# Feed-forward gate and up by Strassen's seven products, over pairs of weight chunks and two groups of tokens

## The chip, the cores and the metric

The kernel runs on one core of one Trainium2 chip. The metric is the device time of one execution in microseconds, here the median of three runs. The engines of the core work side by side and wait for each other through semaphores: PE (TensorE, matrix products), DVE (VectorE), ACT (ScalarE), POOL (GpSimd), and SP (SyncE), which here only issues DMAs.

## The reference

Two layers of an encoder run over 1168 tokens: 1024 of a prompt, 128 of eight running streams and 16 meta tokens. Each layer projects the input, attends in two groups of heads, mixes, and ends with a dense feed-forward part. The change is in that last part alone:

```python
x = layer_norm(ALPHA * x + jnp.einsum('btm,md->btd', mix, w_out), ln1_g, ln1_b)
hid = jax.nn.silu(jnp.einsum('btd,df->btf', x, wg)) * jnp.einsum('btd,df->btf', x, wu)
return layer_norm(ALPHA * x + jnp.einsum('btf,fd->btd', hid, wd), ln2_g, ln2_b)
```

Here `x` is 1168 x 1024, `wg` and `wu` are 1024 x 2816 and `wd` is 2816 x 1024, all in 32 bits.

## The kernel before

Every product of float32 matrices is made of three matmuls in the type float32r, in the helper `three` (lines 2426, 2427 and 2428): each operand is held as a high part, rounded to float32r, and a remainder ("hi" and "lo"), and high x high, high x remainder and remainder x high are added up in PSUM. The first operand that `three` is given is loaded as weights, 128 x 128, the second is moved through. High parts are made by copies on ACT, remainders by subtraction (original minus high part) on POOL or DVE.

The tokens lie transposed, as `xh` and `xl`, 128 features to a partition, in KD = 8 blocks of 1168 columns. The 2816 hidden features are FC = 22 chunks of 128. A turn of the feed-forward loop takes two chunks. For each chunk gate and up are computed for three groups of tokens, N0 and NT (390, 390, 388 columns), each over the eight feature blocks (`up_or_gate`). The results of gate lie in three banks of PSUM and those of up in three others. ACT makes silu of the gate (line 1771), DVE multiplies it by up (line 2359), ACT rounds the product into `hidh` (line 1776), DVE makes `hidl` (line 2363).

Down (`down`) takes both chunks of the turn before: 8 blocks of output by 3 groups of tokens give 24 units of 6 matmuls. Units take turns on the two banks `Tb`; DVE adds each to `acc` in SBUF (line 2381, in the first turn line 2372 with the factor ALPHA). A unit waits for the addition of the unit two before it (semaphore `f_y`).

The order is written out by hand on each engine. On PE a turn is: gate of chunk 0, the down units of the turn before, then up of chunk 0, gate and up of chunk 1. Six weight tiles of 512 KB come for every turn in the order TURN_ITEMS; ACT makes the high part (`weights_hi`), POOL the remainder (`w_lo`, line 1343: 1024 elements to a partition). Of DVE's 36 operations of a turn only the six `hidl` ones read two tensors in SBUF; the others read PSUM and SBUF.

The attention stages ahead use the same split. Line 2116 (DVE) rounds probabilities, and lines 2120 (DVE) and 1288 (POOL) make the two halves of their remainders at the same time, each from two tensors in SBUF.

Of the kernel before, what the change touches and what calls it, by code (L numbers as in the profile page):

```python
# [9 lines left out]
ALU = mybir.AluOpType  # L10
# [86 lines left out]
X_GROUPS = ((0, 1, 2), (3, 4, 5), (6, 7), (8, 9))  # L97
# [167 lines left out]
def program(nc, X, LNP, ROT, W_IN, QKVG, W_UQ, W_UK, W_UV, SINKS, MIXG, W_OUT, LN1, W_FF,  # L265
# [7 lines left out]
    with ExitStack() as ctx:  # L273
# [228 lines left out]
        xh = m("xh", [P, KD, TOK], F32R)  # L502
        xl = m("xl", [P, KD, TOK], F32R)
        after_x = m.at
# [9 lines left out]
        m = Map(common)  # L514
        m.at = after_x
        acc = m("acc", [P, KD, TOK])

        hidh, hidl, fwh, fwl = [None] * 2, [None] * 2, [None] * 6, [None] * 6
        for i in range(2):
            hidh[i], hidl[i] = m(f"hidh{i}", [P, TOK], F32R), m(f"hidl{i}", [P, TOK], F32R)  # L520

        late_end = win_at + W_LATE * 4 * INW
        fwh[4] = m("fwh4", [P, KD, P], F32R)
        assert m.at <= late_end
        for i in range(2):
            fwh[i], fwl[i] = m(f"fwh{i}", [P, KD, P], F32R), m(f"fwl{i}", [P, KD, P], F32R)
        gate = m("gate", [P, TOK])
        fwh[2], fwl[2] = m("fwh2", [P, KD, P], F32R), m("fwl2", [P, KD, P], F32R)
        assert m.at >= win_at + KD * 4 * INW
        fwl[4] = m("fwl4", [P, KD, P], F32R)  # L530
        fwh[5], fwl[5] = m("fwh5", [P, KD, P], F32R), m("fwl5", [P, KD, P], F32R)
        assert m.at <= win_at + (KD + W_LATE) * 4 * INW
        fwh[3], fwl[3] = m("fwh3", [P, KD, P], F32R), m("fwl3", [P, KD, P], F32R)
        fraw = [raw[0][:, 0:D].rearrange("p (k f) -> p k f", f=P), raw[1][:, 0:D].rearrange("p (k f) -> p k f", f=P),
                m("fraw2", [P, KD, P])[:, :, :]]

# [157 lines left out]
        LAST_T = (11, 13, 15, 19, 21, 23)  # L694
        LAST_STATS = (12, 14, 16, 20, 22, 23)
# [3 lines left out]
        def last_bank(e):  # L699
            return (Tb[0], Tb[1], PS[:, 2 * BANK:3 * BANK], PS[:, 5 * BANK:6 * BANK])[e % 4]  # L700
# [232 lines left out]
        def _(sp):  # L933
            for l in range(L):
# [19 lines left out]
                if l >= 1:  # L954
# [4 lines left out]
                    sp.wait_ge(S("f_lo"), W_ITEMS * l)  # L959
# [2122 lines left out]
```

## Time and profile before

| | |
|---|---|
| median of three runs | 3252.19 us (3252.14 to 3256.39) |
| span of the profiled execution | 3254.4 us |
| PE busy | 3060.8 us, 94% |
| DVE, ACT, POOL busy | 1445.3, 895.4 and 835.9 us |
| feed-forward stretch of layer 1, about 2362 to 3226 us | 864 us |

Busy times are sums over the span; an engine that is busy for 44% of it can still be the one that another waits for in some stage. Matmuls are pipelined: a row's duration is longer than the distance from its start to the next one's, which is what a sequence of them costs.

### The profile page before, as it was taken

To read this page: it belongs to the slowest core of one execution; us is meant where nothing else is said; L and a number is where in the kernel's file an instruction comes from. 1 tells how busy PE (TensorE), PEld (TensorE's weight loads), DVE (VectorE), ACT (ScalarE), POOL (GpSimd) and SP (SyncE) were. 2 spreads that over 40 slices of the span, in tenths; PEclk is the share of its full clock that TensorE was granted. 3 is DMA by queue.
4 is the path that set the end of the run, shared out by engine and by line. 5 is a ranking of instruction groups with operands and counts; after the bars stand their busy time and mean duration, and the time that the engine had idled before them with its cause. 6 is when DMAs were issued, how large, how long until landed. Compare 5 with 4: busy or idle time off the path is not lost. (4 is left out here: it accounts for less than half of the span.)

```text
span 3254.4 us, 46316 instructions
## 1 busy us (share of the span) xinstructions
PE 3060.8 (94%) x18352; PEld 2792.0 (86%) x18352; DVE 1445.3 (44%) x2763; ACT 895.4 (28%) x1726; POOL 835.9 (26%) x684
## 2 busy tenths in 40 slices
PE   7979998999999999999889699989899999999997
PEld 6956666878999999999889566678699999999996
DVE  6657776653222222222454677766422222222225
ACT  3333344434111111111233344354431111111111
POOL 2323343421111211111432234434121111111113
PEclk9979998999999999999989899989999999999998
DMA  4321115633111111110232212065321111111101
GB/s 169 131 74 48 40 34 163 181 106 115 39 45 39 39 45 39 39 39 26 105 107 98 73 43 56 18 206 170 103 89 46 39 39 39 39 39 39 39 26 72
DMA packets 143826, 235.36 MB, mean 72 GB/s; under 512 B 52528, under 2 KB 93744, under 8 KB 143376
## 3 DMA queue, kind: packets, MB, share of 16 engines
q1 hardware_dynamic: 133120, 202.48, 19.5%
q0 software_dynamic: 10576, 31.14, 2.5%
q8 instruction: 84, 1.38, 0.2%
q14 instruction: 46, 0.38, 0.0%
HBM read 179.13 MB, written 50.38 MB: 71 GB/s over the span
## 5 line engine op out<-in xcount | busy, mean ns | idle before, releaser
L2427 PE MATMUL PS<-xl,fwh 128*128 128x390 f32 (+1 forms) x2112 | 721.9, 342 | 0.0
L2426 PE MATMUL PS<-xh,fwh 128*128 128x390 f32 (+1 forms) x2112 | 720.3, 341 | 0.6
L2428 PE MATMUL PS<-xh,fwl 128*128 128x390 f32 (+1 forms) x2112 | 720.7, 341 | 0.0
L2381 DVE TENSOR_TENSOR acc<-acc,PS 128x390 f32<-128x390 f32 (+1 forms) x432 | 241.7, 560 | 420.8 <-PE PS L2428 420.8
L2359 DVE TENSOR_TENSOR gate<-PS,gate 128x390 f32<-128x390 f32 x132 | 74.3, 563 | 739.7 <-PE PS L2428 739.7
L2426 PEld LDWEIGHTS PS<-xh,fwh 128*128 128x128 f32 x2112 | 399.1, 189 | 3.1 <-DVE xl L2279 2.5
L2427 PEld LDWEIGHTS PS<-xl,fwh 128*128 128x128 f32 x2112 | 398.5, 189 | 0.4
L2428 PEld LDWEIGHTS PS<-xh,fwl 128*128 128x128 f32 x2112 | 398.6, 189 | 0.0
L2426 PE MATMUL PS<-hidh,fwh 128*128 128x390 f32 (+1 forms) x1056 | 359.0, 340 | 5.2 <-DVE hidl L2363 4.5
L2428 PE MATMUL PS<-hidh,fwl 128*128 128x390 f32 (+1 forms) x1056 | 360.5, 341 | 0.0
L2427 PE MATMUL PS<-hidl,fwh 128*128 128x390 f32 (+1 forms) x1056 | 358.9, 340 | 0.0
L1776 ACT ACTIVATE hidh<-gate 128x390 fp32r<-128x390 f32 x132 | 70.0, 531 | 990.6 <-DVE gate L2359 990.6
L1343 POOL TENSOR_TENSOR fwl<-raw,fwh 128x1024 fp32r<-128x1024 f32 x82 | 195.8, 2397 | 544.2 <-ACT fwh L1788 446.8
L1288 POOL TENSOR_TENSOR Pl<-Pf,Ph 128x256 fp32r<-128x256 f32 (+5 forms) x174 | 219.0, 1265 | 393.3 <-DVE Ph L2116 393.3
L1343 POOL TENSOR_TENSOR fwl<-fraw,fwh 128x1024 fp32r<-128x1024 f32 x42 | 100.4, 2391 | 774.9 <-ACT fwh L1793 674.5
L1587 ACT ACTIVATE Pf<-PS 128x512 f32<-128x512 f32 (+5 forms) x174 | 127.6, 752 | 284.4 <-PE PS L2535 283.9
L2426 PEld LDWEIGHTS PS<-hidh,fwh 128*128 128x128 f32 x1056 | 199.0, 188 | 6.4 <-issue 5.0
L2428 PEld LDWEIGHTS PS<-hidh,fwl 128*128 128x128 f32 x1056 | 199.7, 189 | 0.0
L2427 PEld LDWEIGHTS PS<-hidl,fwh 128*128 128x128 f32 x1056 | 198.7, 188 | 0.0
L2426 PE MATMUL PS<-winh,xTh 128*128 128x394 f32 (+3 forms) x480 | 170.4, 355 | 9.6 <-DVE xTl L1863 5.6
L2427 PE MATMUL PS<-winl,xTh 128*128 128x394 f32 (+3 forms) x480 | 166.3, 347 | 0.0
L2428 PE MATMUL PS<-winh,xTl 128*128 128x394 f32 (+3 forms) x480 | 166.1, 346 | 0.0
(442 smaller groups left out, 5364.3 us busy)
## 6 DMA issues: line engine op xcount, KB each, us to landing
raw<-in_W_FF SPq DMA_DIRECT2D x88, 512.0 KB, 3.3
fraw<-in_W_FF SPq DMA_DIRECT2D x44, 512.0 KB, 3.2
sqt_scratch<-sqTs POOLq DMA_DIRECT2D x18, 512.0 KB, 4.6
hc<-out_H SPq DMA_DIRECT2D x18, 512.0 KB, 3.5
out_H<-yo POOLq DMA_DIRECT2D x18, 512.0 KB, 3.0
dkraw<-in_CKVT SPq DMA_DIRECT2D x16, 520.0 KB, 4.5
QS<-sqt_scratch SPq DMA_DIRECT2D x16, 512.0 KB, 3.4
mt<-mix_scratch SPq DMA_DIRECT2D x16, 512.0 KB, 4.7
```

The source lines that it names most:

```text
L1288: ins = pool.tensor_tensor(Pl[i][0:kk, 1, c], Pf[i][0:kk, 1, c], f(Ph[i][0:kk, 1, c]), ALU.subtract)
L1343: pool.tensor_tensor(fwl[dst][:, :, :], fraw[slot], f(fwh[dst][:, :, :]), ALU.subtract)\
L1587: ins = act.activation(Pf[r][0:kk, :, c], both_banks(u)[0:kk, :, c], ACT.Exp)
L1776: act.activation(hidh[c][:, N0[i]:N0[i] + NT[i]], gate[:, N0[i]:N0[i] + NT[i]], ACT.Copy)\
L2359: dve.tensor_tensor(g, u_bank(i), g, ALU.mult).then_inc(S("f_hid"), 1)
L2381: dve.tensor_tensor(a, a, Tb[e % 2][:, 0:NT[i]], ALU.add).then_inc(S("f_y"), 1)
L2426: pe.matmul(out, wh, mh, start=start, stop=False)
L2427: pe.matmul(out, wh, ml, start=False, stop=False)
L2428: return pe.matmul(out, wl, mh, start=False, stop=stop)
```

## The change

Gate and up are no longer computed chunk by chunk. A pair is now chunk p and chunk p + 11. The weights of a pair are seen as a 2 x 2 matrix of blocks (two halves of the 1024 features by two chunks), the tokens as another (two halves of a group's tokens by two halves of the features). Strassen's form (Winograd's variant) then gives the four blocks of the result from seven products of half-size blocks instead of eight. Its operands are X_OP and W_OP: some are blocks, the others (S1 to S4, T1 to T4) sums and differences of blocks, made on DVE. Every operand is split into a high part and a remainder after it has been summed.

The tokens are in two groups, of 512 and 656, so matmuls move half a group, 256 or 328 columns. All eleven pairs are run for the first group, then all for the second, 22 turns in all; the weights are loaded, summed and split anew for each. A turn has 14 products of 4 x 3 matmuls (7 of gate, 7 of up) in the banks BANK_OF, and 16 down units of 6 matmuls for the turn before. All 16 stand behind product 6, between gate and up (DOWN_STEPS). The x operands of the second group are made in turns 10 and 11, in the places of those of the first.

On DVE `product_sum` and `quarter_sum` add products in PSUM to partial sums in SBUF (`sum_u`, `upper`, `gate`) and multiply up by silu of gate; `w_sum` makes T1 to T4 for gate and for up; `hid_lo` makes the remainders of hid in two operations. On POOL `w_lo` and `down_lo` make 18 remainders of 512 elements a turn. BANK_READER names the DVE operation after which a product's bank is free.

On DVE, in the feed-forward loop of before (`hidl` is the remainder of hid, `acc` the sum in SBUF, `PS` any PSUM):

```order
L2363 TENSOR_TENSOR hidl0_260<-gate_268,hidh0_259 128x390 [waits f_hidh] x2
L2363 TENSOR_TENSOR hidl0_260<-gate_268,hidh0_259 128x388 [waits f_hidh]
L2359 TENSOR_TENSOR gate_268<-PS,gate_268 128x390 [waits f_up,f_silu] x2
L2359 TENSOR_TENSOR gate_268<-PS,gate_268 128x388 [waits f_up,f_silu]
...
L2381 TENSOR_TENSOR acc_258<-acc_258,PS 128x390 [waits f_down]
...
L2381 TENSOR_TENSOR acc_258<-acc_258,PS 128x390 [waits f_down]
...
L2381 TENSOR_TENSOR acc_258<-acc_258,PS 128x388 [waits f_down]
```

and in the loop of the first token group after, from the second up product on (`T1` to `T4` are the weight sums, `rg0` and `rg1` hold the pair's gate weights for the next turn; the T3 row reads two halves of `rg1`):

```order
L2604 TENSOR_TENSOR upper_294<-PS,sum_u0_291 128x256 [waits f_acted,f_prod]
...
L2607 TENSOR_TENSOR gate_295<-upper_294,gate_295 128x256 [waits f_acted]
...
L2562 TENSOR_TENSOR T1_302<-rg1_312,rg0_311 128x512 [waits f_g_in]
...
L2562 TENSOR_TENSOR T2_303<-rg1_312,T1_302 128x512 [waits f_t]
L2580 TENSOR_TENSOR sum_u1_292<-PS,sum_u0_291 128x256 [waits f_prod]
...
L2562 TENSOR_TENSOR T3_308<-rg1_312 128x512 [waits f_g_in,f_lo]
...
L2583 TENSOR_TENSOR sum_u2_293<-PS,sum_u1_292 128x256 [waits f_made]
...
L2562 TENSOR_TENSOR T4_309<-rg0_311,T2_303 128x512 [waits f_t]
...
L2604 TENSOR_TENSOR upper_294<-PS,sum_u2_293 128x256 [waits f_made]
...
L2607 TENSOR_TENSOR gate_295<-upper_294,gate_295 128x256 [waits f_acted]
```

Between two sums out of PSUM now stand operations that read SBUF alone. In the same place before stood additions to `acc` only, each behind a wait for its down unit.

On POOL, one turn of before (`fraw`, `raw` hold raw weights):

```order
L1343 TENSOR_TENSOR fwl0_265<-raw1_69,fwh0_264 128x1024 [waits f_hi]
...
L1343 TENSOR_TENSOR fwl4_271<-fraw2_276,fwh4_263 128x1024 [waits f_hi]
...
L1343 TENSOR_TENSOR fwl5_273<-raw0_68,fwh5_272 128x1024 [waits f_hi]
...
L1343 TENSOR_TENSOR fwl1_267<-raw1_69,fwh1_266 128x1024 [waits f_hi]
...
L1343 TENSOR_TENSOR fwl2_270<-fraw2_276,fwh2_269 128x1024 [waits f_hi]
...
L1343 TENSOR_TENSOR fwl3_275<-raw0_68,fwh3_274 128x1024 [waits f_hi]
```

and part of a turn after, from the first up product on (`wopl` is the remainder of a product's weights, `wdl` that of down):

```order
L1470 TENSOR_TENSOR wopl0_279<-rg0_311,woph0_278 128x512 [waits f_hi]
...
L1470 TENSOR_TENSOR wopl1_281<-rg0_311,woph1_280 128x512 [waits f_hi]
...
L1470 TENSOR_TENSOR wopl2_283<-T2_303,woph2_282 128x512 [waits f_hi]
...
L1477 TENSOR_TENSOR wdl_297<-rd0_310,wdh_296 128x512 [waits f_dhi]
...
L1477 TENSOR_TENSOR wdl_297<-rd1_305,wdh_296 128x512 [waits f_dhi]
...
L1470 TENSOR_TENSOR wopl3_285<-T1_302,woph3_284 128x512 [waits f_hi]
...
L1470 TENSOR_TENSOR wopl4_287<-T3_308,woph4_286 128x512 [waits f_hi]
...
L1470 TENSOR_TENSOR wopl5_299<-T4_309,woph5_298 128x512 [waits f_hi]
...
L1470 TENSOR_TENSOR wopl6_301<-rg1_312,woph6_300 128x512 [waits f_hi]
...
L1470 TENSOR_TENSOR wopl0_279<-ru0_306,woph0_278 128x512 [waits f_hi]
```

Six operations of 1024 elements a turn have become eighteen of 512, four of them (`wdl`, in two pairs) between the weights of the products.

On PE, the first down unit of before:

```order
L2426 MATMUL PS<-xh_248,fwh3_274 128x388 [waits f_hid]
L2427 MATMUL PS<-xl_249,fwh3_274 128x388
L2428 MATMUL PS<-xh_248,fwl3_275 128x388
L2426 MATMUL PS<-xh_248,fwh3_274 128x388
L2427 MATMUL PS<-xl_249,fwh3_274 128x388
L2428 MATMUL PS<-xh_248,fwl3_275 128x388
L2426 MATMUL PS<-xh_248,fwh3_274 128x388
```

and the end of the seventh product and the first two and a half down units after:

```order
L2730 MATMUL PS<-xoh6_254,woph6_300 128x256 [waits f_acted]
L2731 MATMUL PS<-xol6_261,woph6_300 128x256
L2732 MATMUL PS<-xoh6_254,wopl6_301 128x256
...
L2730 MATMUL PS<-hidh_289,wdh_296 128x256 [waits f_made]
L2731 MATMUL PS<-hidl_290,wdh_296 128x256
L2732 MATMUL PS<-hidh_289,wdl_297 128x256
L2730 MATMUL PS<-hidh_289,wdh_296 128x256
L2731 MATMUL PS<-hidl_290,wdh_296 128x256
L2732 MATMUL PS<-hidh_289,wdl_297 128x256
L2730 MATMUL PS<-hidh_289,wdh_296 128x256 [waits f_y]
```

The unit's own shape is the same, two chunks of three matmuls; it is 256 columns wide, and the third one, 12 matmuls on, waits for the first addition (`f_y`).

The diff, cut to its core; the constants, then POOL's turn:

```diff
-TURNS = FC // 2
-TURN_ITEMS = [(1, 0, 0), (0, 0, 2), (0, 1, 2), (1, 0, 1), (1, 1, 0), (1, 1, 1)]
-NT = (390, 390, 388)
-N0 = (0, 390, 780)
+PAIRS = FC // 2
+TURNS = 2 * PAIRS
+PRODUCTS = 14
+DOWNS = 16
+G_TOKENS = (4 * P, TOK - 4 * P)
+HALF_G = (G_TOKENS[0] // 2, G_TOKENS[1] // 2)
+X_OP, W_OP = ("A11", "A12", "S2", "S1", "S3", "A22", "S4"), ("B11", "B21", "T2", "T1", "T3", "T4", "B22")
+BANK_OF = (0, 1, 2, 3, 4, 5, 0, 1, 2, 3, 4, 5, 2, 3)
+DOWN_STEPS = (6,) * 16
...
+                def turn(j, c, downs=True, ahead=True):
+                    for i in range(PRODUCTS):
+                        if i < 7 or ahead:
+                            w_lo(j, c, i + 7)
+                        if i == 1 and downs:
+                            down_lo(j - 1, c, 1)
+                        if i == 9:
+                            down_lo(j, c, 0)
```

ACT's copies of the weights:

```diff
+                def w_hi(j, c, i, first=False):
+                    w, k = i // 7, i % 7
+                    if not first:
+                        act.wait_ge(S("f_prod"), Q(j, c, PRODUCTS, i - 6))
...
+                    if name[0] == "T":
+                        act.wait_ge(S("f_t"), Q(j, c, 8, 4 * w + int(name[1])))
```

DVE:

```diff
+                def hid_lo(j, c, g):
+                    for h in (1, 0):
+                        dve.wait_ge(S("f_acted"), acted(j, c, "hi1" if h else "hi0"))
+                        dve.tensor_tensor(hidl[:, :, half_of(g, h)], gate[:, :, half_of(g, h)],
+                                          f(hidh[:, :, half_of(g, h)]), ALU.subtract).then_inc(S("f_made"), 1)
+                def product_sum(j, c, g, i):
...
+                    if m == 2:
+                        dve.tensor_tensor(u2, product, u1, ALU.add).then_inc(S("f_made"), 1)
...
+                    if m == 4:
+                        dve.wait_ge(S("f_made"), made(j, c, "UV"[w] + "4"))
+                        quarter_sum(j, c, g, w, 1, product, u4)
+                        dve.tensor_tensor(u1, product, u2, ALU.add).then_inc(S("f_made"), 1)
...
+                def turn(j, c, g, no=None):
...
+                    for i in range(PRODUCTS):
+                        if i == 0 and not first:
+                            hid_lo(j - 1, c, before)
...
+                        if i == 1:
+                            w_sum(j, c, 1, 1)
+                            w_sum(j, c, 1, 2)
+                        if i % 7:
+                            product_sum(j, c, g, i)
...
+                        if i in (3, 4):
+                            w_sum(j, c, 1, i)
+                        if i == 8 and not last:
+                            w_sum(j, c, 2, 1)
+                            w_sum(j, c, 2, 2)
+                        if i in (9, 10) and not last:
+                            w_sum(j, c, 2, i - 6)
+                        for u in range(DOWNS):
+                            if DOWN_STEPS[u] == i and not first:
+                                down_add(j - 1, c, before, u, scaled)
```

PE:

```diff
+                def product(j, c, g, i, no):
...
+                    for k in range(4):
+                        ins = three(w_bank(i, g), woph[m][:, k, :], wopl[m][:, k, :],
+                                    x_op(xoh[m], g)[:, k, :], x_op(xol[m], g)[:, k, :],
+                                    k == 0, k == 3)
+                    ins.then_inc(S("f_prod"), 1)
...
+                    for i in range(PRODUCTS):
+                        product(j, c, g, i, no)
+                        for u in range(DOWNS):
+                            if DOWN_STEPS[u] == i and not first:
+                                if no == 1 and u < 2:
+                                    pe.wait_ge(S("c_x1"), 2 * KD * (l + 1))
+                                else:
+                                    pe.wait_ge(S("f_y"), Q(j - 1, c, DOWNS, u - 1))
+                                e, h = down_of(u)
+                                down(j - 1, c, before, u, down_bank(u, before), e, h)
```

## Rows read from the trace of the kernel before

**Rows 1.** The page, parts 1 and 2

```profile
PE 3060.8 (94%) x18352; PEld 2792.0 (86%) x18352; DVE 1445.3 (44%) x2763; ACT 895.4 (28%) x1726; POOL 835.9 (26%) x684
...
PE   7979998999999999999889699989899999999997
...
PEclk9979998999999999999989899989999999999998
...
GB/s 169 131 74 48 40 34 163 181 106 115 39 45 39 39 45 39 39 39 26 105 107 98 73 43 56 18 206 170 103 89 46 39 39 39 39 39 39 39 26 72
```

**Rows 2.** Busy us by stretch: length, engines (instructions), clock, DMA share, GB/s

```profile
2435.90:2461.40 25.50, 25.50 (x145) 25.50 (x145) 12.87 (x23) 1.44 (x2) 2.41 (x1) 1.00 0.06 21
2461.40:2512.70 51.30, 51.30 (x289) 51.27 (x289) 6.78 (x13) 10.41 (x16) 11.88 (x5) 1.00 0.16 52
```

**Rows 3.** The page, part 5: group xcount | busy us, mean ns | idle

```profile
L2427 PE MATMUL PS<-xl,fwh 128*128 128x390 f32 (+1 forms) x2112 | 721.9, 342 | 0.0
...
L1343 POOL TENSOR_TENSOR fwl<-raw,fwh 128x1024 fp32r<-128x1024 f32 x82 | 195.8, 2397 | 544.2 <-ACT fwh L1788 446.8
```

**Rows 4.** Timeline of all engines at 1000 us: start, us, instruction [idle before]

```profile
999.76 0.34 PE L2426 MATMUL PS<-hidh,fwh 128*128 128x390 f32 x1
...
1000.65 0.34 PE L2428 MATMUL PS<-hidh,fwl 128*128 128x390 f32 x1
...
1001.02 0.56 DVE L2381 TENSOR_TENSOR acc<-acc,PS 128x390 f32<-128x390 f32 x1 [0.51 <-PE PS L2428]
...
1003.83 0.34 PE L2428 MATMUL PS<-hidh,fwl 128*128 128x390 f32 x1
```

**Rows 5.** Timeline of PE at 1814 us and at 2340 us

```profile
1814.67 0.28 PE L2428 MATMUL PS<-wuqh,cqT 128*128 128x256 f32 x1
...
1815.39 0.28 PE L2428 MATMUL PS<-wuqh,cqT 128*128 128x256 f32 x1
...
2340.26 0.40 PE L2427 MATMUL PS<-woutl,mT8h 128*128 128x512 f32 x1
...
2345.40 0.40 PE L2428 MATMUL PS<-wouth,mT8l 128*128 128x512 f32 x1
```

**Rows 6.** DVE's groups by shape

```profile
L2120 DVE TENSOR_TENSOR Pl<-Pf,Ph 80x256 fp32r<-80x256 f32 x32 | 29.5, 923 | 0.1
...
L2120 DVE TENSOR_TENSOR Pl<-Pf,Ph 128x256 fp32r<-128x256 f32 x44 | 18.7, 425 | 1.5
...
L2031 DVE SCALAR_TENSOR_TENSOR QNl<-PS,QNh 128x512 fp32r<-128x512 f32 x16 | 11.1, 691 | 6.1 <-ACT QNh L1549 5.7
...
L2339 DVE TENSOR_TENSOR fwl<-raw,fwh 128x1024 fp32r<-128x1024 f32 x6 | 7.3, 1225 | 10.8 <-ACT fwh L1383 10.8
...
L1939 DVE TENSOR_TENSOR cqT<-PS,cqT 128x256 fp32r<-128x256 f32 x16 | 6.7, 420 | 44.6 <-ACT KR L1464 44.6
```

**Rows 7.** POOL's and ACT's groups by shape

```profile
L1288 POOL TENSOR_TENSOR Pl<-Pf,Ph 128x512 fp32r<-128x512 f32 x48 | 84.9, 1769 | 99.2 <-DVE Ph L2116 99.2
...
L1788 ACT ACTIVATE fwh<-raw 128x1024 fp32r<-128x1024 f32 x60 | 63.0, 1049 | 0.0
```

**Rows 8.** Lines 2120 and 1288 around 237 us: ns min/median/max, starts

```profile
L2120 DVE TENSOR_TENSOR Pl<-Pf,Ph x2: 418/685/952, 236.5 to 236.9; 64x256 fp32r<-64x256 f32 x1, 80x256 fp32r<-80x256 f32 x1
...
L1288 POOL TENSOR_TENSOR Pl<-Pf,Ph x2: 912/938/965, 236.6 to 237.5; 64x256 fp32r<-64x256 f32 x1, 80x256 fp32r<-80x256 f32 x1
```

**Rows 9.** Timeline of DVE and of POOL, 2096.5 to 2100.5 us

```profile
2097.26 2.89 DVE L2120 TENSOR_TENSOR Pl<-Pf,Ph 128x512 fp32r<-128x512 f32 x1
...
2095.99 3.61 POOL L1288 TENSOR_TENSOR Pl<-Pf,Ph 16x512 fp32r<-16x512 f32 x2 [3.84 <-DVE Ph L2116]
```

**Rows 10.** Timeline of PE, 3192.5 to 3199 us

```profile
3193.37 0.41 PE L2426 MATMUL PS<-hidh,fwh 128*128 128x390 f32 x1 [2.23 <-DVE hidl L2363]
...
3194.95 0.53 PE L2428 MATMUL PS<-hidh,fwl 128*128 128x390 f32 x1
...
3198.19 0.34 PE L2426 MATMUL PS<-hidh,fwh 128*128 128x390 f32 x1
```

More of the change, by code:

```diff
@@ new lines, in program @@
+        acc0 = m("acc0", [P, KD, G_TOKENS[0]])
+        early_at = m.at
+        woph = [m(f"woph{i}", [P, 4, P], F32R) if a == 0 else m(f"wopl{i}", [P, 4, P], F32R) for i in range(5) for a in range(2)]
+        woph, wopl = woph[0::2], woph[1::2]
+        assert m.at <= 139712
+        xin.append(Map(126912)("xin3", [P, D]))
+        m = Map(139712)
+        hid_at = m.at
+        hidh = m("hidh", [P, 2, G_TOKENS[1]], F32R)
+        hidl = m("hidl", [P, 2, G_TOKENS[1]], F32R)
+        sums_u = [m(f"sum_u{i}", [P, HALF_G[1]]) for i in range(3)]
@@ L1355, in _ @@
+                first_root(9)
+                for i in range(4, 7):
+                    w_lo(0, c, i, True)
+                turn(0, c, downs=False)
+                with pool.Fori(1, 2 * PAIRS - 1) as j:
+                    turn(j, c)
+                turn(TURNS - 1, c, ahead=False)
+                down_lo(TURNS - 1, c, 1)
                 if l + 1 < L:
-                    pool.wait_ge(S("f_lo"), W_ITEMS * (l + 1))
+                    pool.wait_ge(S("f_lo"), PRODUCTS * TURNS * (l + 1))
+                    pool.wait_ge(S("f_dlo"), 4 * TURNS * (l + 1))
@@ new lines, in down_hi @@
+                def down_hi(j, c, s, first=False):
+                    for n in range(2):
+                        act.wait_ge(S("f_d_in"), Q(j, c, 64, 32 * s + 32))
+                        if first and s == 0:
+                            act.wait_ge(S("c_hT"), XT(l, 1, KD - 1) + 1)
+                        elif not first:
+                            act.wait_ge(S("f_down"), Q(j, c, DOWNS, 8 * s - 8))
+                        act.activation(wdh[:, n, 4 * s:4 * s + 4, :], rd[n][:, :, :], ACT.Copy).then_inc(S("f_dhi"), 1)
@@ L2329, in _ @@
                 mix_norm(9)
-                for k in range(4):
-                    x_lo(0, k)
                 mix_lo(9)
@@ L2964, in _ @@
[L2964 to L2972 removed]
+                for k in range(4, KD):
+                    x_T(0, k)
+                w_out(9, 0, KD)
@@ new lines, in down @@
+                def down(j, c, g, u, out, e, h):
+                    if u == 0:
+                        pe.wait_ge(S("f_dlo"), Q(j, c, 4, 2))
+                        pe.wait_ge(S("f_made"), made(j, c, "lo0"))
+                    if e == 4:
+                        pe.wait_ge(S("f_dlo"), Q(j, c, 4, 4))
+                    for n in range(2):
+                        ins = three(out, wdh[:, n, e, :], wdl[:, n, e, :], hidh[:, n, half_of(g, h)], hidl[:, n, half_of(g, h)],
+                                    n == 0, n == 1)
+                    ins.then_inc(S("f_down"), 1)
```

755 lines of the change are left out of this document (464 added, 291 removed).

## The prediction

> **What bounds the kernel now.** I read the page's busy times and slices first, then the busy time by stretch, then the costliest groups, and last the timeline of TensorE. PE is busy 94% of the span, and the slices show two plateaus in which it is full and the clock is granted whole [rows 1]. These are the feed-forward parts. One turn of their loop there is a stretch of 25.5 us of down projection and one of 51.3 us of gate and up, both with PE busy to the last tenth while DVE, ACT and POOL are at most half busy [rows 2]. So TensorE's issue rate is the bound, and the three remainder products of each matmul (6336 for gate and up, 3168 for down) are the work (three lines with 2112 each for gate and up over both layers [rows 3], three with 1056 for down). In the loop nothing waits on DVE: each addition of a down unit (0.56 us) starts 0.37 us after the unit's last matmul starts, and DVE then idles 0.5 us [rows 4]. The 342 ns that the groups give as a mean is a pipelined duration; what counts is the pitch. From 999.76 to 1003.83 us there are 23 pitches of 390 columns: 0.177 us each [rows 4].
>
> **What the matmuls cost after the change.** Token groups of 512 and 656 are halved, so matmuls move 256 and 328 columns. Six pitches of 256 columns take 0.72 us: 0.120 us each [rows 5]. 512 columns take (2345.40 - 2340.26)/22 = 0.234 us [rows 5]. For 328 I go straight from 256 to 390: 0.120 + 72/134 x 0.057 = 0.151 us. Bounds for 328: 0.120 and 0.177, the rows on either side; straight lines between three points leave less than 0.003 of real doubt.
> Before, a layer has 3168 + 1584 = 4752 matmuls: 4752 x 0.177 = 841 us. After, gate and up are 11 pairs x 14 products x 12 = 1848 for each token group, down 11 x 16 units x 6 = 1056 for each: 2904 x 0.120 + 2904 x 0.151 = 787 us. That is **-54 us a layer**: an eighth of the 561 us of gate and up is 70, and the narrower matmuls give 16 back.
> The Trainium skill (TensorE: Matmul & The Clock Gate, section "Wait — 56ns, not 53.3ns?") has the gap of warm matmuls as the columns at 2.4 GHz plus 2.5 ns, so 0.109 us for 256 and 0.165 for 390. The rows show 0.120 and 0.177; each matmul here has its own weight load. By the page the saving would be about 63 us a layer. I take the rows.
>
> **What the change adds on the other engines.** Per turn (one pair, one token group), by the order and by durations of like operations:
> DVE, from PSUM: 18 product sums of which 4 are SBUF only, so 14, and 16 down additions, of 256 or 328 columns: 0.42 us at 256 and 0.56 at 390 [rows 4, 6], so 0.50 at 328. From SBUF with two SBUF inputs: 4 multiplications by the gate (0.42 / 0.50), 8 weight sums T1 to T4 of 512 (0.69, as the 512-wide row) and 2 hid remainders of 512 or 656 (0.69 / 0.84, between the 512 and 1024 rows). Sum: 12.6 + 1.7 + 5.5 + 1.4 = 21 us of a 31.7 us turn (264 x 0.120), 25 us of 39.9 (264 x 0.151). By busy time alone DVE fits.
> POOL: 18 remainders of 512. 1024 take 2.39 us [rows 3, 7]; 512 beside a DVE operation take 1.77, of which 0.65 is the wait told below [rows 7], so 1.12 to 1.20 alone; I take 1.15: 21 us. ACT: 18 copies of 512 at half of 1.05 plus overhead, 0.6 [rows 7], and 8 small ones: 15 us, never late. SP loads the weights once for each token group, 3.1 MB a turn: 99 GB/s in 31.7 us, where slices of before move up to 206 [rows 1]; each load is asked for some 15 us ahead of its first reader. That costs nothing; if it did, T1 would be the reader that waits.
> The down block itself: two banks, so unit u+2 waits for the addition of u. Last matmul start + 0.32 (0.37 at 390, less 0.05) + 0.42 + 0.05 = 0.79 us, and the unit is due at 7 x 0.120 = 0.84. It holds by 0.05; nothing to 0.3 us a turn is lost, I take 0.2.
>
> **The term that decides: POOL and DVE don't run beside each other.** In the attention part the 80-row remainder of 256 columns takes 0.92 us on DVE, the 128-row one 0.42 [rows 6]. At 236.5 us is why: DVE starts its first at once (0.42), POOL's takes 0.96 because it waits for that; DVE's second then takes 0.95, waiting for POOL, and POOL's second again 0.91 [rows 8]. Two instructions that each read two SBUF tensors take turns. Additions out of PSUM are not held: they keep their 0.56 us. In the feed-forward part of before, DVE has such an operation only in hidl, when POOL idles; after, 14 a turn meet POOL's 18. The Trainium skill (SBUF — State Buffer, section "Who interferes with whom") says it as a rule: a DVE instruction with two SBUF inputs contends with a GpSimd instruction that reads SBUF, and the one that is late blocks fully. The rows above agree; it is the rule that speaks against this change.
> A walk through one turn, time 0 at the start of the first up product (1.44 us each in the 512 group), a held DVE operation at 0.55 (512) or 0.28 (256) once it is let in, each POOL one at 1.15. ACT copies sum and silu, then the first weight: POOL can start at 3.1. It alternates with DVE: two remainders, the product h11, T1, T2: 3.1 + 2.35 + 0.28 + 0.55 + 0.7 = 7.0. POOL's third waits for T2 to be copied (0.6) and for T3 on DVE: done 9.1. From there POOL always has work: two down remainders, four up-phase ones, two of the next gate phase and two down ones, 10 x 1.15 = 11.5 us; between them DVE in its fixed order does T4, three multiplications, two hid remainders, and T1 to T4 of the next up weights: 5 x 0.55 + 3 x 0.28 + 2 x 0.55 = 4.7 us. That is 25.3; then product sums five and six (0.8) and the first down addition (0.5): **26.6 us**. PE wants that addition after 7 + 7 products and two units: 20.2 + 1.4 = 21.6. So PE waits 5.0 us at the third down unit, in every turn of the 512 group. In the 656 group the same walk gives 28.2 (POOL's part is unchanged, DVE's 0.9 longer, ACT's 0.4) against 25.4 + 1.8 = 27.2: 1 us.
> The waiting PE also loses clock: before the last turn's down PE stood 2.23 us, and from 3194.95 to 3198.19 us ten pitches are 0.324 instead of 0.177 [rows 10]: 1.5 us, 1.6 with the one before. I add that to each 5 us wait.
> Per layer: 10 blocks x (5.0 + 1.6 + 0.2) = 68; 11 x 1 = 11; the change of token groups puts 12 operations of 1312 elements on DVE (1.22 us at 1024 [rows 6], so 1.5): 18 us, all before an already late block; the start (11 DVE operations of 1024 against 11 us of w_out cover and the first products) and the end (two sums, a copy and a remainder ahead of the last down) 6. Sum +103 - 54 = **+49 a layer, +98 in all**. The bounds of the wait are zero (an idle POOL whenever DVE comes) and 13.5 us a turn (rival 2); the walk's own error I put at 2.5 us a turn.
> The profiled execution spans 3254.4 us, 2 us over the median of the three timed runs (3252.19). 3254.4 + 98 - 2 = **3350 us**. The walk's error over 21 turns a layer makes the case's own range 3270 to 3430.
>
> **Rivals.**
> 1. PE stays the bound (faster). For it: PE was never short of DVE or POOL in the loop [rows 2, 4], DVE needs only two thirds of a turn, and each hold may fall into DVE's idle time. Against: the walk has POOL with work waiting from 9 to 25 us. It gives -108, +24 for start, change of group and end, +4 for the blocks: 3172 us. It decides if the first down addition comes before 21.6 us.
> 2. POOL keeps the port as long as its next instruction is already issued (much slower). At 2097.3 us DVE's 512 took 2.89 us, through the end of one POOL instruction and all of the next [rows 9]; and two such against some 38 cases of taking turns (32 of them the 80-row form of [rows 6]). Then T4 waits until POOL runs dry at 14.5, PE loses 4.5 us on banks, and the first addition comes at 34: +13.5 and +9 us a turn, with the clock 15 and 10.7: 10 x 15 + 11 x 10.7 + 24 - 54 = +238 a layer: 3730 us.
> 3. The change does less than it says: narrower matmuls are bound by weight loads, not columns. The 256-column pitch already contains that [rows 5], so at most the 328 one could: at 0.177 a layer costs 76 us more, 22 over before: 3296 us with nothing else. Chance 0.02.
>
> **Chances.** The taking of turns with a late block 0.66, PE-bound 0.24, the port kept 0.08, the weight loads 0.02. The range reaches down to rival 1 and leaves rival 2 out: 3165 to 3450. A difference of 0.2% (6.5 us) is what the runs can tell from none. Faster: rival 1 and the low end of the walk's error, 0.25; within 0.2%: 0.03; slower 0.72.
>
> **What would show it.** Right: the pitch in the down block 0.120 and 0.151; POOL's 512 remainders at 1.15 to 1.8 us with a mean near 1.5, T sums on DVE near 1.2 rather than 0.69; PE idle about 5 us before the third down unit of the 512 group, ended by an addition on acc0, with the granted clock under 1 behind it, and about 1 us in the 656 group. Wrong: these sums at 0.69, or PE busy through the block (rival 1); T sums of 3 us and more (rival 2); a pitch of 256 columns that isn't 0.120.

## The result, and the profile after

The changed kernel takes 3347.88 us (median of four runs, 3344.71 to 3356.53), the kernel before 3254.29 us beside it: 1.029 times as long (95% interval 1.0274 to 1.0303). The forecast was 3350 us. The profiled execution spans 3354.6 us.

From the page, parts 1, 2 and 5 (columns as in [rows 1, 3]):

```profile
PE 2996.7 (89%) x20464; PEld 2718.0 (81%) x20464; DVE 2345.6 (70%) x3913; ACT 1206.5 (36%) x2390; POOL 1736.2 (52%) x1352
...
PE   7979998987889879999889799889789997899997
...
PEclk9989998998999989999989799989899998999998
...
L2730 PE MATMUL PS<-hidh,wdh 128*128 128x256 f32 (+1 forms) x1408 | 449.6, 319 | 91.9 <-DVE acc L2618 74.4
```

PE is busy 64 us less than before, and yet the span of the profiled execution is 100 us longer (94 us by the medians). The plateaus of [rows 1] have turned into a pattern of eights and nines, most of all in the first half of each feed-forward part; the last row says what PE waits for there: 74 us for additions on `acc`.

Busy time by stretch in layer 0 (length, engines with instructions, clock, DMA share, GB/s): the start up to the second turn, the ten turns of the first token group, the change of groups, ten turns of the second group, and the end.

```profile
743.60:787.10 43.50, 20.27 (x133) 18.10 (x133) 37.15 (x47) 17.51 (x26) 20.97 (x14) 0.76 0.26 99
787.10:1158.60 371.50, 335.97 (x2642) 331.08 (x2642) 277.34 (x441) 130.61 (x261) 267.47 (x181) 0.95 0.26 89
1158.60:1217.50 58.90, 39.59 (x266) 38.62 (x266) 49.58 (x56) 21.61 (x33) 32.52 (x18) 0.83 0.16 54
1217.50:1623.80 406.30, 400.09 (x2642) 397.19 (x2641) 307.77 (x440) 139.02 (x260) 273.30 (x180) 1.00 0.21 72
1623.80:1663.40 39.60, 34.76 (x230) 33.63 (x228) 25.58 (x50) 11.10 (x14) 19.39 (x13) 0.96 0.44 176
...
1010.20:1030.30 20.10, 20.08 (x171) 19.87 (x170) 17.01 (x20) 9.25 (x18) 15.22 (x11) 1.00 0.11 35
1030.30:1047.30 17.00, 13.49 (x98) 13.18 (x97) 10.74 (x25) 3.78 (x8) 11.32 (x9) 0.90 0.42 148
```

At the pitches of 0.120 and 0.151 us the matmuls of these five stretches need 10.1, 316.8, 34.3, 398.6 and 27.2 us. So 33, 55, 25, 8 and 12 us are something else. The last two rows are one turn of the first group: its 14 products run full, its down block has PE busy for 13.5 of 17.0 us at a clock of 0.90 and holds all of the turn's loss.

TensorE in that block (start, duration, [idle before]):

```profile
1031.54 0.28 PE L2732 MATMUL PS<-hidh,wdl 128*128 128x256 f32 x1
1035.32 0.57 PE L2730 MATMUL PS<-hidh,wdh 128*128 128x256 f32 x1 [3.51 <-DVE acc L2618]
...
1038.46 0.41 PE L2732 MATMUL PS<-hidh,wdl 128*128 128x256 f32 x1
...
1038.85 0.28 PE L2731 MATMUL PS<-hidl,wdh 128*128 128x256 f32 x1
```

Twelve matmuls into the block PE stands until the first addition on `acc`, as forecast: 3.8 us from one start to the next, 3.7 us more than the pitch, where 5 us were forecast. Then 14 matmuls come at 0.214 us each instead of 0.120; the granted clock from 1035.4 to 1038.6 us is 0.50, the lower level of 1.2 GHz. Not every such block pays for that: with the same wait, three of the twenty take 15.6 us, five 17.8 to 18.2 and the others 17.0 or 17.1. DVE over the same time:

```profile
1023.95 3.51 DVE L2567 TENSOR_TENSOR hidl<-gate,hidh 128x512 fp32r<-128x512 f32 x2
1027.38 1.77 DVE L2562 TENSOR_TENSOR T<-ru,ru 128x512 f32<-128x512 f32 x1
1029.19 1.68 DVE L2562 TENSOR_TENSOR T<-ru,T 128x512 f32<-128x512 f32 x1
1030.80 0.41 DVE L2601 TENSOR_TENSOR gate<-PS,sum_u 128x256 f32<-128x256 f32 x1
...
1031.91 0.68 DVE L2562 TENSOR_TENSOR T<-ru 128x512 f32<-128x512 f32 x1
...
1033.18 1.09 DVE L2562 TENSOR_TENSOR T<-ru,T 128x512 f32<-128x512 f32 x1
1034.19 0.74 DVE L2601 TENSOR_TENSOR gate<-PS,sum_u 128x256 f32<-128x256 f32 x2
1034.86 0.74 DVE L2618 TENSOR_TENSOR acc<-acc,PS 128x256 f32<-128x256 f32 x2
```

There is no idle time in it. All but one of the operations that read SBUF alone take 1.1 to 1.8 us, where the 512-wide one of [rows 6] takes 0.69; that row reads PSUM too, but a_fill below gives the same 0.68 to 0.69 for the sums themselves. The exception is T3, which keeps its 0.68: it starts just as POOL goes from one instruction to the next (POOL's start at 1031.99). The sums out of PSUM between them keep their 0.41. By shape, over the kernel (busy us, mean ns | idle), first DVE, then POOL:

```profile
L2562 DVE TENSOR_TENSOR T<-ru,T 128x512 f32<-128x512 f32 x88 | 117.4, 1334 | 2.7
...
L2562 DVE TENSOR_TENSOR T<-ru,ru 128x512 f32<-128x512 f32 x44 | 78.2, 1778 | 0.0
L2607 DVE TENSOR_TENSOR gate<-upper,gate 128x256 f32<-128x256 f32 x88 | 73.6, 836 | 7.3
L2567 DVE TENSOR_TENSOR hidl<-gate,hidh 128x512 fp32r<-128x512 f32 x44 | 72.5, 1687 | 0.0
...
L2491 DVE TENSOR_TENSOR xol<-acc,xoh 128x1312 fp32r<-128x1312 f32 x6 | 13.5, 2245 | 0.0
```

```profile
L1470 POOL TENSOR_TENSOR wopl<-T,woph 128x512 fp32r<-128x512 f32 x348 | 502.2, 1467 | 109.7 <-ACT woph L1912 109.7
L1477 POOL TENSOR_TENSOR wdl<-rd,wdh 128x512 fp32r<-128x512 f32 x176 | 285.1, 1640 | 40.7 <-ACT wdh L1921 40.7
```

### The profile page after: what moved, and what is told of

Same layout as the page of the kernel before. It is cut to its first block and busy times, and to the rows that moved or that the text cites. A ratio compares the mean times of both kernels' runs of the same rounds, so it can differ in the third digit from the quotient of the medians.

```text
span 3354.6 us, 58492 instructions
## 1 busy us (share of the span) xinstructions
PE 2996.7 (89%) x20464; PEld 2718.0 (81%) x20464; DVE 2345.6 (70%) x3913; ACT 1206.5 (36%) x2390; POOL 1736.2 (52%) x1352
## 5 line engine op out<-in xcount | busy, mean ns | idle before, releaser
L2730 PE MATMUL PS<-xoh,woph 128*128 128x256 f32 (+1 forms) x2464 | 742.2, 301 | 45.0 <-issue 28.9
L2732 PE MATMUL PS<-xoh,wopl 128*128 128x256 f32 (+1 forms) x2464 | 738.5, 300 | 0.0
L2731 PE MATMUL PS<-xol,woph 128*128 128x256 f32 (+1 forms) x2464 | 737.3, 299 | 0.0
L1470 POOL TENSOR_TENSOR wopl<-T,woph 128x512 fp32r<-128x512 f32 x348 | 502.2, 1467 | 109.7 <-ACT woph L1912 109.7
L2730 PE MATMUL PS<-hidh,wdh 128*128 128x256 f32 (+1 forms) x1408 | 449.6, 319 | 91.9 <-DVE acc L2618 74.4
L2730 PEld LDWEIGHTS PS<-xoh,woph 128*128 128x128 f32 x2464 | 469.0, 190 | 52.1 <-issue 51.3
L2732 PEld LDWEIGHTS PS<-xoh,wopl 128*128 128x128 f32 x2464 | 469.8, 191 | 0.0
L2731 PEld LDWEIGHTS PS<-xol,woph 128*128 128x128 f32 x2464 | 469.6, 191 | 0.0
L2731 PE MATMUL PS<-hidl,wdh 128*128 128x256 f32 (+1 forms) x1408 | 433.9, 308 | 0.0
L2732 PE MATMUL PS<-hidh,wdl 128*128 128x256 f32 (+1 forms) x1408 | 433.6, 308 | 0.0
```

Source lines behind the costliest of these rows:

```text
L1470: pool.tensor_tensor(wopl[k][:, :, :], w_whole(w, k, first), f(woph[k][:, :, :]), ALU.subtract)\
L2730: pe.matmul(out, wh, mh, start=start, stop=False)
L2731: pe.matmul(out, wh, ml, start=False, stop=False)
L2732: return pe.matmul(out, wl, mh, start=False, stop=stop)
```

## The experiments

Theory: POOL's remainders and DVE's operations that read SBUF alone take turns, which makes the first down addition late; PE waits for it and then runs at half clock. Rivals: DVE's list is too long by itself; the single down block is what overruns DVE; a chain of the weight sums binds.

**POOL without its reads (a_fill, 3 rounds).**

```diff
-pool.tensor_tensor(wopl[k][:, :, :], w_whole(w, k, first), f(woph[k][:, :, :]), ALU.subtract)
+pool.tensor_tensor(wopl[k][:, 0, 0:2], w_whole(w, k, first)[:, 0, 0:2], f(woph[k][:, 0, 0:2]), ALU.subtract)
+for b in range(1, 4):
+    for h in range(2):
+        pool.memset(f(wopl[k][:, b, 64 * h:64 * h + 64]), 0.0)
+pool.memset(f(wopl[k][:, 0, 2:P]), 0.0)
```

and the same for `wdl`. The kernel leaves out the remainders but for two columns and fills the tiles with zeros, which reads nothing.

> The remainders on POOL (weights of products and of down, 18 a turn) are left out but for two columns: POOL fills the tiles with zeros instead, in seven memsets that read nothing, of 64 and 126 elements (98 to 204 ns each for such sizes in the trace: 0.8 to 1.2 us with the small subtraction, against 1.28 us for a remainder that nothing holds). DVE's list is unchanged. Theory (port): DVE is held because POOL reads SBUF at the same time; then T sums fall to about 0.69 us and hidl to 0.69 and 0.84 us, the gap before the third down unit of the first group goes (3.78 us to 0.12 us), a turn takes 32 us instead of 37.1 and 40.0 instead of 40.6, and the kernel 3348 - 20 x 5.1 - 20 x 0.7 - 2 x 8 (change of groups) = 3215 us (3195 to 3240). Rival (DVE's list ahead of the first down addition is too long by itself): T sums stay at 1.1 to 1.8 us or the first down addition stays late, 3345 us.

Measured: 3193.9 us (3187.34 to 3196.78), 0.981 of the kernel before (0.9788 to 0.9836). DVE's T sums (ns min/median/max), and one turn of the first group:

```profile
L2568 DVE TENSOR_TENSOR T<-ru,T x88: 679/691/709, 766.1 to 3102.8; 128x512 f32<-128x512 f32 x88
...
L2568 DVE TENSOR_TENSOR T<-ru,ru x44: 677/683/687, 765.3 to 3095.8; 128x512 f32<-128x512 f32 x44
```

```profile
1034.00:1065.70 31.70, 31.70 (x267) 31.55 (x266) 20.22 (x44) 13.30 (x26) 16.68 (x144) 1.00 0.29 99
```

The most numerous of POOL's memsets, in the same view:

```profile
L1473 POOL MEMSET wopl<- x3696: 141/148/155, 741.4 to 3106.9; 128x64 f32 x195
```

The T sums now lie between 0.68 and 0.71 us, DVE does the same 44 operations of a turn in 20.2 instead of 27.8 us, PE has no gap, and a turn takes 31.7 us, the matmuls' own time. The change of groups falls from 58.9 to 47.4 us. The rival (DVE's list by itself) is out. One reserve: the fill keeps POOL busy for 16.7 us a turn, less than the 23 us (18 x 1.28) of remainders that nothing holds, so it takes away some POOL time along with the reads. What it shows of the reads stands in the single rows: POOL is busy for half of the turn, and yet neither side is held: DVE's sums stay within 0.67 and 0.72 us and the memsets within 0.014 us of each other; only the two-column subtractions, which read, still take up to 1.6 us.

**POOL with one input (j_poolcopy), DVE with one input (k_dvecopy), 1 round each.** j fills the remainders, but for two columns, by copies of the high parts (`pool.tensor_copy`). k leaves out the weight sums:

```diff
-dve.tensor_tensor(out[:, :, :], a, b, ALU.subtract).then_inc(S("f_t"), 1)
+dve.tensor_copy(out[:, :, :], a).then_inc(S("f_t"), 1)
```

> As a_fill, but POOL fills the remainders (but for two columns) with copies of the high parts, so that it reads one SBUF tensor instead of two or none. If reading at all is what holds DVE: T sums on DVE stay above 0.9 us and some wait is left at the third down unit. If only two inputs on POOL hold DVE: T sums at 0.69 us, turns of 31.7 and 39.8 us as in a_fill, 3194 us if POOL is in time.

> The weight sums T1 to T4 are left out: DVE copies the first of their two inputs instead (one SBUF input, eight a turn); multiplications and hid remainders on DVE and all of POOL stay. If only operations of DVE with two SBUF inputs take turns with POOL: the copies aren't held (0.5 us or less), the four ahead of the down block give back 3 us and more, the gap before the third down unit falls from 3.8 to about 0.5 us and the kernel to about 3235 us. If any SBUF-only operation is held: the copies take 1 us and more on average and the kernel stays over 3300 us.

Measured: j 3200.01 us (two runs), k 3274.2 us (three runs). The same groups in j, then in k:

```profile
L2564 DVE TENSOR_TENSOR T<-ru,T x88: 680/777/992, 766.8 to 3116.5; 128x512 f32<-128x512 f32 x88
...
L2564 DVE TENSOR_TENSOR T<-ru,ru x44: 677/680/769, 766.0 to 3109.7; 128x512 f32<-128x512 f32 x44
```

```profile
L2562 DVE COPY T<-ru x176: 416/1408/1531, 770.3 to 3188.1; 128x512 f32<-128x512 f32 x176
```

By its time and its turns (31.7 and 39.8 us, as in a_fill) j looks like the second case of its expectation, that only two inputs on POOL hold DVE. The rows of the two engines say otherwise. In j, in order of time:

```profile
1047.37 0.68 DVE L2564 TENSOR_TENSOR T<-ru,ru 128x512 f32<-128x512 f32 x1
1047.45 0.97 POOL L1471 CAST wopl<-woph 128x384 fp32r<-128x384 f32 x1
1048.09 0.88 DVE L2564 TENSOR_TENSOR T<-ru,T 128x512 f32<-128x512 f32 x1
...
1049.22 0.49 POOL L1471 CAST wopl<-woph 128x384 fp32r<-128x384 f32 x1
```

The copy that starts behind a sum takes 0.97 us instead of 0.49, and the next sum, which starts while that copy runs, 0.88 instead of 0.68: they take turns as before. Over the kernel such a copy takes 0.50 us at the least and at the median and up to 1.80; the T sums go up to 1.08. So POOL's copies with one input do take turns with DVE's sums. They cost DVE only a tenth of a microsecond at the median because it now waits for instructions of 0.2 to 0.5 us instead of 1.28; that reading fits the rows, but j has less POOL work as well (20.2 us of a turn, its holds included), and no run keeps POOL's time and shortens its instructions.

Copies on DVE, which have one input, are held too: 0.42 us free, and those of up's weights 1.41 at the median. So k kept more of its wait (1.9 us of idle before the third unit) than the two-input reading of the theory gave it, and 3274 lies between its two expectations. I had worded the condition as two inputs on both sides; that was too narrow on both.

**The list ahead of the first addition (b_late_T, 3 rounds), the banks (c_banks, 3 rounds), both (d_both, 3 rounds).** In b, T3 and T4 of up move into the block:

```diff
-if i in (3, 4):
+if first and i in (3, 4):
     w_sum(j, c, 1, i)
...
 down_add(j - 1, c, before, u, scaled)
+if u in (9, 13):
+    w_sum(j, c, 1, 3 + (9, 13).index(u))
```

In c, down takes turns on four banks; PE waits for the addition four units back, and products 7 and 8 for the last two:

```diff
-return Tb[u % 2][:, 0:HALF_G[g]]
+return (Tb[0], Tb[1], PS[:, BANK:2 * BANK], PS[:, 2 * BANK:3 * BANK])[u % 4][:, 0:HALF_G[g]]
...
-pe.wait_ge(S("f_y"), Q(j - 1, c, DOWNS, u - 1))
+pe.wait_ge(S("f_y"), Q(j - 1, c, DOWNS, u - 3))
```

> DVE's T3 and T4 for up move from steps 3 and 4 to behind the down additions of units 9 and 13. Theory (the first down addition is late because shared operations of DVE stand ahead of it): 0.68 + 1.10 us leave the stretch ahead of it, the wait before the third down unit falls from 3.7 to about 1.9 us and the clock loss behind it from 1.7 to about 1, a turn of the first group takes 34.6 us, one of the second 39.9 to 40.1: 3348 - 20 x 2.5 - 20 x 0.6 = 3285 us (3265 to 3300). Rival (T3 and T4 come too late for products 12 and 13, a new wait takes the place of the old): 3340 us or more, with a gap in front of the twelfth product. Rival (POOL's backlog and not DVE's list sets the time of the addition): POOL waits for T3 and has less behind it, the gap shrinks by 3 us or more, 3260 us.

> The down block takes turns on four banks instead of two (two banks of products already read); nothing moves on DVE, POOL or ACT. Theory (only the lateness of DVE's additions stops PE): the fifth instead of the third unit is the first to wait, due 1.4 us later, so 3.7 us of wait become 2.2, in the second group 0.8 becomes 0: 3348 - 20 x 2 - 20 x 0.8 = 3290 us (3275 to 3310). Rival (DVE as a whole is the bound, 29.3 us busy in a 37.1 us turn with its own waits): the wait moves to the product behind the block, which needs the last addition: 3340 us.

> Both edits: T3 and T4 of up inside the down block, and four banks. Theory (lateness of the first addition alone): 3.7 - 1.8 - 1.4 leaves 0.4 us, a turn of the first group 32.2 us, of the second 40.0: 3348 - 20 x 4.9 - 20 x 0.7 = 3236 us (3220 to 3260), under the 3254 us of the kernel before. Rival (DVE and POOL taking turns don't fit into a 32 us turn: DVE was busy for 29.3 us with its holds): a turn stays at 34 us or more and the kernel at 3275 us or more.

Measured: b 3297.68 us, c 3281.16 us, d 3254.17 us; ratios to the kernel before 1.0123 (1.0104 to 1.0141), 1.0075 (1.0058 to 1.0092) and 0.9993 (0.9984 to 1.0003). The row of PE's wait in b (third unit), in c (fifth unit) and in d (fifth unit):

```profile
1017.76 0.39 PE L2732 MATMUL PS<-hidh,wdh 128*128 128x256 f32 x1 [2.14 <-DVE acc L2618]
```

```profile
981.49 0.39 PE L2730 MATMUL PS<-hidh,wdh 128*128 128x256 f32 x1 [2.08 <-DVE acc L2618]
```

```profile
1011.69 0.38 PE L2732 MATMUL PS<-hidh,wdh 128*128 128x256 f32 x1 [0.69 <-DVE acc L2618]
```

3.51 us of idle became 2.14 when 1.8 us of DVE's work left the list, 2.08 when PE needed the addition 1.4 us later, and 0.69 with both: the cuts in the wait add up. The gains in time do so only in part, 50 and 67 us alone and 94 together, since either edit by itself already ends the second group's wait and most of the loss of clock. No gap opened at products 12 and 13. Most turns of the first group take 34.5, 33.9 and 32.8 us (with the few slower ones 34.9, 34.2 and 32.8 at the mean), those of the second 39.8 to 40.0. d is as fast as the kernel before, inside what can be told apart.

**The block spread out (h_spread, 3 rounds).**

```diff
-DOWN_STEPS = (6,) * 16
+DOWN_STEPS = (4,) * 5 + (5,) * 5 + (6,) * 6
```

> The sixteen down units of a turn no longer stand in one block behind gate's seventh product: five behind the fifth, five behind the sixth, six behind the seventh (one table of numbers; each engine's order follows). Theory (what is late is DVE's list ahead of the first down addition, with POOL taking turns): nothing is taken from that list but T4 and two product sums (2.3 us), while the addition is wanted 2.9 us earlier; so PE waits before the third down unit for about 3.7 + 0.6 us and in the later groups of units hardly: 3345 to 3375 us. Rival (the single block is what overruns DVE; spread out, the additions fit between product sums): PE stays the bound, 3250 us or less.

Measured: 3511.37 us (3510.79 to 3516.32), 1.079 (1.0769 to 1.0813). PE at the first and the third unit:

```profile
965.73 0.38 PE L2730 MATMUL PS<-hidh,wdh 128*128 128x256 f32 x1 [0.20 <-DVE hidl L2567]
...
972.85 0.58 PE L2730 MATMUL PS<-hidh,wdh 128*128 128x256 f32 x1 [5.44 <-DVE acc L2618]
```

The direction is the theory's, the size was mine to get wrong by more than a hundred microseconds: T4 still stands ahead of the first addition, only two sums (0.8 us) leave, and the addition is wanted 2.9 us earlier, so 3.7 - 0.8 + 2.9 = 5.8 us of waiting. A turn of the first group takes 38.8 us for 37.1; one of the second 45.0 for 40.6, and that group, for which the expectation had nothing, has more than half of the loss. Against this spread, the single late block is the better order, and it isn't what overruns DVE.

**The start (f_start, 3 rounds).** SP asks for the first gate weights ahead of the last store and load of the residual; ACT:

```diff
-w_hi(0, c, 0, True)
 x_op_hi(0, 0)
-w_hi(0, c, 1, True)
 x_op_hi(0, 1)
+w_hi(0, c, 0, True)
+w_hi(0, c, 1, True)
```

> The first gate weights are asked for ahead of the store and load of the last residual rows, and ACT rounds the first two token operands before the first weights; else the kernel is the changed one. Theory (the start of the feed-forward part is bound by DVE's list, which begins 9.7 us after acc0 is there, at 744.98 instead of 735.3 us, because ACT waits for a weight load first): PE's standstill from 754.7 to 768.7 us shrinks by 7 to 9 us in each layer: 3348 - 2 x 8 = 3332 us (3326 to 3340). Rival (DVE then waits for first weights or for the last w_out rows in the middle of its list): 3342 us or more.

Measured: 3336.72 us (3332.1 to 3343.55), 11 us less than the changed kernel. By the whole time that is not clear of noise: the ratios to the kernel before, 1.0251 (1.0222 to 1.0279) and 1.0288 (1.0274 to 1.0303), overlap. The place itself shows it. ACT in the changed kernel, its DVE, and then DVE in this one:

```profile
743.30 0.63 ACT L1912 ACTIVATE woph<-rg 128x512 fp32r<-128x512 f32 x1 [11.03 <-DMA first_rg<-in_W_FF]
```

```profile
744.98 3.61 DVE L2491 TENSOR_TENSOR xol<-acc,xoh 128x1024 fp32r<-128x1024 f32 x2 [9.84 <-ACT xoh L1849]
```

```profile
734.85 2.34 DVE L2491 TENSOR_TENSOR xol<-acc,xoh 128x1024 fp32r<-128x1024 f32 x2
```

The list begins 10 us earlier, and the turn that follows starts at 779.0 instead of 787.1 us, 8.1 us earlier; in layer 1 the same stretch is 7.7 us shorter.

**All together (e_three, g_all, i_groups, 3 rounds each; l_last, 5 rounds).** e is c with T2, T3 and T4 made after units 5, 9 and 13 (a table `T_LATE = {2: 5, 3: 9, 4: 13}`, and a wait on DVE's own last `hidl` in T2's old place). g adds the earlier start. i makes S4 at the change of groups in one operation instead of two. l is i with T4 after unit 15:

```diff
-("lo0", "lo1", "S1", "S2", "S3", "lo2", "lo3", "lo4", "lo5", "part", "S4", "lo6")
+("lo0", "lo1", "S1", "S2", "S3", "S4", "lo2", "lo3", "lo4", "lo5", "lo6")
...
-T_LATE = {2: 5, 3: 9, 4: 13}
+T_LATE = {2: 5, 3: 9, 4: 15}
```

> Four banks, and T2, T3 and T4 of up behind the down additions of units 5, 9 and 13. Theory (lateness of the first addition): in d_both 0.85 us of wait are left at the fifth unit, T2 (1.1 to 1.7 us) moves behind it, so no wait is left in the block: 11.7 us instead of 12.6, the turn 31.9 us instead of 32.8: 3254 - 20 x 0.9 = 3236 us (3225 to 3248). Rival (a chain instead: T2, its copy and its remainder come too late for product 9, 2.9 us behind the block): 3250 us or more and a gap ahead of the tenth product.

> Four banks, three late T sums and the earlier start together. If the three losses are separate the gains add up: 3236 - 16 = 3220 us (3205 to 3235), 1% under the kernel before. If the start only shifts work (rival), 3236 us.

> Four banks, three late T sums, the earlier start, and at the change of token groups the operand S4 made as A12 - S2 before the remainder of S2 takes its place, instead of A12 less S2's high part less its remainder afterwards: one operation of 1312 elements less on DVE (2.2 to 2.5 us with POOL's turns), and the last one leaves the path of the seventh product, which waited 7.4 us for it. Theory (the change of groups is bound by DVE's list): the 45.1 us of that turn's products fall by 3 to 5 us in each layer, 3230 - 8 = 3222 us (3216 to 3226). Rival (POOL or ACT bound there): 3229 us.

> As i_groups, but T4 of up is made behind the last down addition of the block instead of behind that of unit 13. In i_groups the product behind the block starts 1.3 us after the matmul before it, since T4 (1.35 us beside POOL) stands ahead of the additions of units 14 and 15, whose banks or counts it waits for. Theory (DVE's order at the end of the block): that gap goes, the block of the first group takes 11.5 to 11.6 us instead of 12.4, the second group is unchanged: 3229 - 20 x 0.9 = 3211 us (3205 to 3218). Rival (T4 then comes too late for product 12, 7 us behind the block): a gap there and 3229 us or more.

Measured: e 3247.81, g 3230.18, i 3229.06 and l 3218.87 us; ratios 0.9976 (0.9963 to 0.9989), 0.992 (0.9896 to 0.9944), 0.9923 (0.9903 to 0.9943), 0.9889 (0.9869 to 0.9909). The last beats both kernels, the one before by 1.1%. For e the rival came closer than the theory (3236 us), though not by its mechanism: the wait inside the block is gone, but 1.1 us opened behind it, at the first product of up, so that a turn takes 32.6 us where d's takes 32.8. No gap of a chain shows ahead of the tenth product. The row, in i, where it is the same:

```profile
1068.66 0.38 PE L2736 MATMUL PS<-xoh,woph 128*128 128x256 f32 x1 [1.04 <-DVE acc L2619]
```

i's gain of 1 us is below what can be told; its change of groups fell by only 1.2 us, to 43.9 us for the products, since the wait before the third product grew while that before the seventh shrank. For l the mechanism in the expectation fell. A turn of the first group, products and block, in i and then in l:

```profile
1036.10:1056.30 20.20, 20.19 (x169) 20.00 (x170) 16.63 (x22) 10.61 (x22) 17.72 (x13) 1.00 0.27 83
1056.30:1068.70 12.40, 11.36 (x99) 11.17 (x97) 10.88 (x23) 2.66 (x6) 7.63 (x7) 1.00 0.33 119
```

```profile
1034.30:1055.50 21.20, 20.96 (x169) 20.16 (x169) 18.56 (x23) 10.91 (x22) 18.09 (x12) 1.00 0.26 77
1055.50:1066.90 11.40, 11.40 (x99) 11.22 (x97) 9.48 (x22) 2.09 (x4) 7.68 (x7) 1.00 0.37 133
```

The block is short by 1.0 us and the products are longer by 1.0, in short gaps ahead of the third, fourth, sixth and seventh product of gate: 32.6 us both times. That looks like the rival of d_both, at 32.6 and not at 34 us: DVE, 27.5 and 28.0 us busy, and POOL, 25.4 and 25.8 us, leave little room, and a wait taken away at one place came back at another. Why it does so at those products was not tested.

So l's edit is not shown to gain anything. Its second group is 1.0 us a layer faster and its change of groups 1.6 us slower, and from the first product to the last down matmul the feed-forward parts of both layers take 1712.3 us in i and 1712.8 us in l. The 4.5 us by which l's span is shorter (3216.5 against 3221.0) stand outside them, in parts that are the same code in both.

## Why the prediction was right, step by step

Times per layer, forecast against layer 0 of the trace (stretches above, less the matmuls' time; from the 33 and 12 us of start and end go 22 us that the same part of before stood beyond its 841 us of matmuls, and 10 us of transposes that have moved there out of the w_out part):

| term | forecast | measured |
|---|---|---|
| matmuls | -54 | -54 at the same pitches |
| first group, ten turns | +68 | +55 |
| second group, ten or eleven turns | +11 | +8 |
| change of groups | +18 | +25 |
| start and end | +6 | +14 |
| sum | +49 | +47 (layer 1: +50) |

- The pitches hold: 168 matmuls of products in 20.1 us are 0.120 us each, in the second group 25.3/168 = 0.151.
- The deciding term was right in mechanism and place, and a_fill shows it by cause. The forecast had POOL without a break from 9.1 to 25.3 us after the first up product; the trace has it from 1019.12 to 1035.40, which is 8.9 to 25.2. The Trainium skill (SBUF — State Buffer, section "Who interferes with whom") was on the right side here.
- That its end comes at 25.2 and not elsewhere is partly luck. A remainder that nothing holds takes 1.28 us, not 1.15, so ten take 12.8 instead of 11.5; DVE's ten operations between them held POOL for 3.5 instead of 4.7 us.
- The step that was mis-sized is its end: I put POOL's last remainder ahead of T4 and the last sums. T4 was let in before it and ended at 24.1, the sums from PSUM ran beside it, and the addition ended at 25.1 instead of 26.6: a wait of 3.7 us instead of 5.0. The clock took 14 x 0.094 = 1.3 us instead of 1.6, the two-bank rhythm about 0.4 instead of 0.2.
- The change of groups was too cheap because I priced its twelve operations at 1.5 us without the turns that the theory itself asks for. They took 2.0 us at the mean, 24 us for the twelve; in a_fill 1.5 each, 18 us.
- Start and end: I counted 11 us of w_out work as cover for DVE's eleven operations. DVE could not begin: ACT waited 11.0 us for gate weights, whose load stood behind SP's last residual transfers, and DVE for ACT. f_start gives back the 8 us that this term lacked.
- Misses of -13, -3, +7 and +8 us a layer cancelled to -2. That the total came within 2 us of the forecast is luck; the parts are good to some 13 us. The stated range was tighter than its own reason: 2.5 us over 42 turns is 105 us each way, not 80.
- DVE's sum for a turn of the second group adds up to 24 us, not 25, and the 0.69 us for a weight sum came from a row that reads PSUM; a_fill confirms the figure.
- Rival 1 needed the addition before 21.6 us; a_fill reaches its place (3194 against 3172 us) only by taking POOL's reads away. Rival 2: T sums never took more than 1.8 us. Rival 3: 328 columns take 0.151 us.
- Layer 1's attention part seemed to end 5 us later than before. That is no more than such a part varies: from the last down matmul of layer 0 to the first product of layer 1 it is 746.0 us here and 739.0 to 750.1 in the eight experiments that leave it untouched. Differences of a few microseconds between spans are to be read with this beside them.

## What to carry to other kernels

Before adding work to DVE and POOL, count as one engine all of POOL's operations that read SBUF and, of DVE's, those with two inputs in SBUF and the copies from SBUF to SBUF. Here the sharing took DVE from 20.2 to 27.8 us of a turn; with POOL's reads, and some of its time, taken away the kernel was 154 us faster, more than the whole loss. Look at the rows of both engines before saying that something isn't held: with short instructions on POOL it was POOL that waited, and DVE's median hardly moved. Put what the waiting engine needs ahead of such work in the list, and give it banks for the lateness that stays; both are cheap to try one at a time. Where an in-order engine starts a new phase, look at which load its first instruction waits for and what stands ahead of that load in its queue.

## What the runs showed of the hardware

- DVE's one-input copy of 512 float32 elements is held by POOL's two-input subtraction (0.42 us free, median 1.41 for those of up's weights in k); its operations with one input in PSUM are not (0.41 to 0.42 us). The Trainium skill (SBUF — State Buffer, section "Who interferes with whom") names copies in a two-port mode as contending; the trace agrees that these copies contend, and no row says in which mode they run.
- POOL's copies, with one SBUF input, take turns with DVE's two-input sums: 384 elements take 0.50 us free and up to 1.80 held, the sums up to 1.08 instead of 0.68. POOL's memsets, which read nothing, neither hold nor are held (0.141 to 0.155 us, sums 0.68 to 0.71). The Trainium skill (SBUF — State Buffer, section "Who interferes with whom") has it that a DVE instruction with two SBUF inputs contends with a GpSimd instruction that reads SBUF, and not with one that only writes it; the trace agrees with both.
- After 3.5 us of standstill in the block PE ran 14 matmuls at 1.2 GHz (0.214 us for 256 columns) in most blocks, and in three of twenty none. In b and c, after 2.1 us, it is the other way round: most blocks show none (a block of 14.4 us is 12.3 busy and the wait), and in five and four of twenty there is a loss of 1.4 us or more.
- The 168 matmuls of a turn's products take 19.7 us in a_fill and 19.8 in j and k, against 20.1 to 20.2 in the others. Less is read from SBUF in all three; that this is the cause was not tested.
